# Fox attention scores with zero-padded 128-row queries, earlier copies in two queues, and one pool window on VectorE

## The reference

```
z = rmsnorm(x, g_mix) @ w_in            # 512 q, 512 k, 512 v, 512 pool columns, 8 forget columns
q, k: split in 8 heads of 64, each rms-normed with a gain
c = cumsum(log_sigmoid(f_logit))
s[t, u] = q_t . k_u / 8 + c[t] - c[u]   for u <= t, else -inf     (forgetting attention)
fox = softmax(s) @ v
pool, group g of 4 (128 columns each), w = 2, 4, 8, 16:
    mixed = mean of the last w frames - the frame;  y_g = mixed @ w_pool[g] * pool_scale
h = x + concat(fox, y) @ w_out
```

## Time and profile before

| | us |
|---|---|
| median of 3 runs | 1363.58 (1363.48 to 1363.75) |
| the profiled execution, its own time | 1360.7 |
| its span | 1358.9 |
| TensorE busy | 1316.6 |
| VectorE busy | 762.7 |
| ScalarE busy | 651.2 |
| GpSimd busy | 105.1 |

### The profile page before, as it was taken

The page is one execution under the profiler, slowest core; times in us unless marked ns, Lnnn a source line. Parts: engine busy times, 40 slices in busy tenths (PEclk is TensorE's granted clock), DMA queues, the critical chain, the costliest instruction groups (busy, mean ns, idle before and its releaser), DMA issues.

```text
span 1358.9 us, 16931 instructions
## 1 busy us (share of the span) xinstructions
PE 1316.6 (97%) x6139; PEld 1082.6 (80%) x6139; DVE 762.7 (56%) x834; ACT 651.2 (48%) x894; POOL 105.1 (8%) x163
## 2 busy tenths in 40 slices
PE   7999889999999999999999999999999999999998
PEld 5777768888888888788788888788888887788886
DVE  5646465555564455657655555755556557754444
ACT  5554455444454444455644444644445556644443
POOL 5114100000000000110100000200002002100000
PEclk9999999999999999999999999999999999999999
DMA  9423236555555555455465555555556533555551
GB/s 324 167 69 123 93 124 205 188 191 189 186 165 187 192 188 196 159 198 185 141 222 187 188 187 191 183 185 187 185 186 188 186 106 118 173 190 185 185 188 60
DMA packets 163485, 236.02 MB, mean 174 GB/s; under 512 B 7745, under 2 KB 120569, under 8 KB 163441
## 3 DMA queue, kind: packets, MB, share of 16 engines
q1 hardware_dynamic: 160864, 228.62, 51.8%
q0 software_dynamic: 1840, 4.64, 1.0%
q10 hardware_dynamic: 736, 2.17, 0.4%
HBM read 234.35 MB, written 1.05 MB: 173 GB/s over the span
## 4 chain that ended last, share of the span: by engine, by line
PE 89%; DVE 4%; ACT 2%; POOL 2%; issue 1%; DMA 1%; SPq 0%; DVEq 0%; POOLq 0%; ACTq 0%
PE B L1519 20%; PE B L1521 20%; PE B L1520 20%; PE B L1878 7%; PE B L1880 7%; PE B L1879 7%; PE T L1891 2%; DVE w_lo L976 2%; DMA w_raw<-in_w_in 1%; DVE xt_lo L991 1%; ACT w_hi L527 1%; POOL KT L414 1%; PE B L2048 1%; PE T L1513 0%; ACT xt_hi L540 0%
## 5 line engine op out<-in xcount | busy, mean ns | idle before, releaser
L976 DVE TENSOR_TENSOR w_lo<-w_raw,w_hi 128x2048 fp32r<-128x2048 f32 x217 | 498.7, 2299 | 296.8 <-ACT w_hi L527 296.8
L527 ACT ACTIVATE w_hi<-w_raw 128x2048 fp32r<-128x2048 f32 x217 | 415.6, 1916 | 168.6 <-PE B L1880 127.3
L1519 PE MATMUL B<-w_hi,xt_lo 128*128 128x512 f32 x1200 | 479.5, 400 | 8.8 <-DVE xt_lo L991 4.7
L1521 PE MATMUL B<-w_hi,xt_hi 128*128 128x512 f32 x1200 | 469.1, 391 | 0.0
L1520 PE MATMUL B<-w_lo,xt_hi 128*128 128x512 f32 x1200 | 468.0, 390 | 0.0
L1519 PEld LDWEIGHTS B<-w_hi,xt_lo 128*128 128x128 f32 x1200 | 225.9, 188 | 56.7 <-issue 8.5
L1521 PEld LDWEIGHTS B<-w_hi,xt_hi 128*128 128x128 f32 x1200 | 225.7, 188 | 48.6
L1520 PEld LDWEIGHTS B<-w_lo,xt_hi 128*128 128x128 f32 x1200 | 226.3, 189 | 43.7
L1878 PE MATMUL B<-w_hi,act_lo 128*128 128x512 f32 x400 | 156.3, 391 | 0.0
L1880 PE MATMUL B<-w_hi,act_hi 128*128 128x512 f32 x400 | 155.7, 389 | 0.0
L1879 PE MATMUL B<-w_lo,act_hi 128*128 128x512 f32 x400 | 155.6, 389 | 0.0
(11 more groups left out here) (269 smaller groups left out, 898.3 us busy)
## 6 DMA issues: line engine op xcount, KB each, us to landing
w_raw<-in_ffn_w_gu SPq DMA_DIRECT2D x176, 512.0 KB, 4.6
w_raw<-in_ffn_w_down SPq DMA_DIRECT2D x88, 512.0 KB, 3.9
w_raw<-in_w_gate_up SPq DMA_DIRECT2D x44, 512.0 KB, 4.7
w_raw<-in_conv_w_in SPq DMA_DIRECT2D x24, 512.0 KB, 4.3
w_raw<-in_w_down SPq DMA_DIRECT2D x22, 512.0 KB, 3.8
w_raw<-in_w_in SPq DMA_DIRECT2D x16, 512.0 KB, 7.9
w_raw<-in_w_kv SPq DMA_DIRECT2D x16, 512.0 KB, 4.9
w_raw<-in_w_mem_kv SPq DMA_DIRECT2D x8, 512.0 KB, 4.7
```

The lines of the kernel that those rows point to most:

```text
L527: act.activation(whi[slot][:, :], raw[slot][:, :], ACT.Copy).then_inc(w_hi, 1)
L976: dve.tensor_tensor(wlo[slot][:, :], raw[slot][:, :], whi[slot][:, :].bitcast(F32), ALU.subtract)\
L1519: pe.matmul(bank[:, :], lo[:, k, x], whi[s][:, c], start=first, stop=False)
L1521: return pe.matmul(bank[:, :], hi[:, k, x], whi[s][:, c], start=False, stop=last)
```

## The change

- QT now holds all eight chunks for the Fox heads: chunk `2 c + m` has head `2 c + m` in its own 64 rows and zeros in the others. VectorE writes the zeros at the start; the later zeroing of the same places for the differential attention stays, and its counts on `qz_ok` are 2 higher. `fox_scores` multiplies 128 rows of padded queries by the 128 rows of KT that hold both heads of a pair.
- The queries are taken out by two instructions per engine, each for half of the partitions, and these stand directly behind the evacuation of the keys.
- TensorE makes two fill triples between the scores of heads 0 and 1.
- ScalarE and VectorE take the pool columns out ahead of split 9; ScalarE's squares of the memory rows stand at heads 2 and 3.
- mixT moves to `gpost`, so the first load of `gpost` comes later in GpSimd's queue. The window of 16 frames is made by VectorE (`widest_window`), at i = 4.
- VectorE scales the memory keys behind the attention output.

```diff
...
 win = [kt_hi[:, (PAD + S) * i:(PAD + S) * (i + 1)] for i in range(2)]
+win16 = [Z[:, i, 2 * (PAD + S):3 * (PAD + S)] for i in range(2)]
 wmean = kt_hi[:, 2 * (PAD + S):2 * (PAD + S) + S]
-mixT = QT[:, 4:8, :]
+mixT = gpost[:, :].rearrange("p (g t) -> p g t", g=4)
 
...
 mixed_ok, py_done = sem("pool_mixed"), sem("pool_product")
+mixed16_ok, pads16_ok = sem("widest_window_mixed"), sem("widest_window_pads_zero")
 at_s, at_m, at_x, at_e, at_r, at_c, at_v = (sem("scores_done"), sem("scores_masked"), sem("row_max_ready"),
...
 
-        if b:
-            pool.wait_ge(h_up, 4 * (3 + b - 1) + 4)
+        pool.wait_ge(*((h_up, 4 * (3 + b - 1) + 4) if b else (py_done, 1)))
         pool.dma_start(gpost[:, :], a["norm_g_2"][layer, i].partition_broadcast(P)).then_inc(post_in, 16)
...
         pool.wait_ge(pads_ok, 3)
-        for g, w in enumerate(WINDOWS):
+        for g, w in enumerate(WINDOWS[:3]):
             src = poolT[g]
...
 
-    post_gain(0, 0, 1)
     row_stat("h0")
...
     row_stat("h2")
+    post_gain(0, 0, 1)
     row_stat("h3")
...
         act.activation(dst, FILL[0][:, :], ACT.Copy, scale=RS[:, ST[stat], 0:1]).then_inc(ev_a, 1)
+
+    def fox_queries_out():
+
+        act.wait_ge(ht, 2 * HT_QF + 1)
+        act.wait_ge(qz_ok, 2)
+        for m in range(2):
+            r = slice(m * FOX_DH, m * FOX_DH + FOX_DH)
+            ins = act.activation(qz_g[0][r, m, 0:2, :], T[0][r, :].rearrange("p (c t) -> p c t", c=2), ACT.Copy,
+                                 scale=gains[r, G_QF:G_QF + 1])
+        ins.then_inc(ht_a, 1)
 
...
     evac(EV_IN + 1, 3, Z[:, 0, 512:1024], PAIR[1], "h0")
+    act.wait_ge(gain_ok, 6)
+    fox_queries_out()
     head_square(1, Z[:, :, 512:1024], EV_IN + 1)
     split_at(6)
-    act.wait_ge(gain_ok, 6)
-    heads_out(HT_QF, QT[:, 0:2, :], G_QF)
     mem_round_hi(0)
...
             mem_round_hi(3)
+            fill_evac(0, Z[:, 0, 1024:1536], "h0")
             split_at(9)
-            mem_squares(0)
-            mem_squares(1)
-            fill_evac(0, Z[:, 0, 1024:1536], "h0")
         elif i == 2:
             split_at(10)
+            mem_squares(0)
             act.wait_ge(pt_done, 1)
...
         elif i == 3:
+            mem_squares(1)
             split_at(11)
...
     dve.memset(gains[:, G_ONE:G_ONE + 1], 1.0).then_inc(gain_ok, 1)
+    dve.memset(qz_g[0][FOX_DH:P, 0], 0.0).then_inc(qz_ok, 1)
+    dve.memset(qz_g[0][0:FOX_DH, 1], 0.0).then_inc(qz_ok, 1)
...
         dve.tensor_scalar(dst, FILL[1][:, :], RS[:, ST[stat], 1:2], None, ALU.mult).then_inc(ev_d, 1)
+
+    def widest_window():
+
+        src = poolT[3]
+        for level in range(4):
+            d = 1 << level
+            dst = win16[level % 2]
+            link(dve.tensor_tensor(dst[:, PAD:PAD + S], src[:, PAD:PAD + S], src[:, PAD - d:PAD + S - d], ALU.add))
+            src = dst
+        dve.scalar_tensor_tensor(out=mixT[:, 3, 16:S], in0=src[:, PAD + 16:PAD + S], scalar=1.0 / WINDOWS[3],
+                                 in1=poolT[3][:, PAD + 16:PAD + S], op0=ALU.mult, op1=ALU.subtract)
+        link(dve.tensor_tensor(src[:, PAD:PAD + 16], src[:, PAD:PAD + 16], cnt16[:, 3, :], ALU.mult))
+        dve.tensor_tensor(mixT[:, 3, 0:16], src[:, PAD:PAD + 16], poolT[3][:, PAD:PAD + 16], ALU.subtract)\
+            .then_inc(mixed16_ok, 1)
 
...
     evac(EV_IN + 1, 3, Z[:, 1, 512:1024], PAIR[1], "h0")
+    dve.wait_ge(ht, 2 * HT_QF + 2)
+    for m in range(2):
+        r = slice(m * FOX_DH, m * FOX_DH + FOX_DH)
+        ins = dve.tensor_scalar(qz_g[0][r, m, 2:4, :], T[1][r, :].rearrange("p (c t) -> p c t", c=2),
+                                gains[r, G_QF:G_QF + 1], None, ALU.mult)
+    ins.then_inc(ht_d, 1)
     head_sum(1, FOX_H, FOX_DH)
     split_at(6)
-    heads_out(HT_QF, QT[:, 2:4, :], G_QF)
     head_scale(1, Z[:, :, 512:1024], FOX_H, FOX_DH)
...
         elif i == 1:
+            fill_evac(U_IN + 7, Z[:, 1, 1024:1536], "h0")
             split_at(9)
-            fill_evac(U_IN + 7, Z[:, 1, 1024:1536], "h0")
         elif i == 2:
...
                 .then_inc(pt_out, 1)
+            for w in win16:
+                dve.memset(w[:, 0:PAD], 0.0).then_inc(pads16_ok, 1)
         elif i == 4:
+            dve.wait_ge(pt_out, 2)
+            dve.wait_ge(pads_ok, 3)
+            dve.wait_ge(pads16_ok, 2)
+            widest_window()
             fill_evac(U_MEMKV + 1, nat[:, 1, HALF:D], "mem")
...
             split_at(13)
-            head_scale(2, nat[:, :, HALF:D], MEM_H, MEM_DH)
             dve.wait_ge(pool_hi, 4)
...
     values_out(0, 16, 0, FOX_H, FOX_DH)
+    head_scale(2, nat[:, :, HALF:D], MEM_H, MEM_DH)
     split_at(14)
...
     def fox_scores(i):
-        c, r = i // 2, slice(64 * (i % 2), 64 * (i % 2) + 64)
+        c, q = i // 2, qz_g[0][:, i % 2, i // 2, :]
         if i >= 2:
...
         b = B[i % 2]
-        for q, lo, width in ((0, 0, P), (1, P, S)):
-            pe.matmul(b[:, lo:lo + width], QT[r, c, q * P:q * P + P], KT[r, c, 0:width], start=True, stop=False)
+        for t, lo, width in ((0, 0, P), (1, P, S)):
+            pe.matmul(b[:, lo:lo + width], q[:, t * P:t * P + P], KT[:, c, 0:width], start=True, stop=False)
             ins = pe.matmul(b[:, lo:lo + width], selr[i // 4][:, i % 4, :], cT[:, 0:width], start=False, stop=True)
...
     fox_scores(0)
+    fill(3, 5)
     fox_scores(1)
-    fill(3, 6)
+    fill(5, 6)
     done = 6
...
         if i == 7:
-            pe.wait_ge(mixed_ok, 4)
+            pe.wait_ge(mixed_ok, 3)
+            pe.wait_ge(mixed16_ok, 1)
             pe.wait_ge(in_small, 64)
```

More of the change, by code:

```diff
@@ L480, in _ @@
             pool.memset(qz_g[0][DIFF_DH:P, 0], 0.0).then_inc(qz_ok, 1)
-            pool.wait_ge(qz_ok, 1)
+            pool.wait_ge(qz_ok, 3)
             pool.memset(qz_g[0][0:DIFF_DH, 1], 0.0).then_inc(qz_ok, 1)
-            pool.wait_ge(qz_ok, 2)
+            pool.wait_ge(qz_ok, 4)
             row_stat("h6")
@@ L495, in _ @@
             pool.memset(qz_g[1][DIFF_DH:P, 0], 0.0).then_inc(qz_ok, 1)
-            pool.wait_ge(qz_ok, 3)
+            pool.wait_ge(qz_ok, 5)
             pool.memset(qz_g[1][0:DIFF_DH, 1], 0.0).then_inc(qz_ok, 1)
-            pool.wait_ge(qz_ok, 4)
+            pool.wait_ge(qz_ok, 6)
             for p in range(4):
@@ L869, in queries_out @@
                 act.wait_ge(ht, 2 * (HT_QD + g) + 1)
-                act.wait_ge(qz_ok, 2 * g + 2)
+                act.wait_ge(qz_ok, 2 * g + 4)
                 for m in range(2):
@@ L1379, in queries_out @@
                 dve.wait_ge(ht, 2 * (HT_QD + g) + 2)
-                dve.wait_ge(qz_ok, 2 * g + 2)
+                dve.wait_ge(qz_ok, 2 * g + 4)
                 for m in range(2):
```

## The result

| | before | after |
|---|---|---|
| median of the runs, us | 1363.53 (1360.56 to 1363.75, 4 runs) | 1347.08 (1345.53 to 1347.95, 4 runs) |
| ratio | | 0.9881, 95% interval 0.9856 to 0.9905 |
| profiled execution, us (span, mean granted clock) | 1360.7 (1358.9, 0.998) | 1346.8 (1345.0, 0.997) |

The kernel is 16.5 us faster by the medians. Between the two profiled executions the difference is 13.9 us; the sum had 13.5. The direction was right, and the sum came close by errors that offset each other; what failed is the step from the profiled execution to the median, and one term was mis-sized (W).

What follows compares the result with a forecast made beforehand. TensorE, busy 97% of the span, bounds the kernel. 2.7 + 6.2 + 3.1 + 1.6 + 0.4 + 1.0 - 1.5 = 13.5 us off 1360.7 gives 1347.2, median 1350.1; own range 1348.5 to 1352, stated range 1347.5 to 1355.0.

Steps and rivals of the forecast that it cites:

- W: Added TensorE wait for the memory key bank copy, behind VectorE's window sum: 1.5 us lost, bounds 0 and 4.
- term D: Iteration 2, from 83.21 us: no clock fall once the 3.11 us idle stretch ahead goes, 1.6 us gained, bounds 0 and 1.7.
- A: Fox query copies moved directly behind the key evacuation: TensorE's gap before 50.70 goes, 2.7 us, bounds 1.5 and 2.9.
- C: Value copy moved ahead of the weight split: TensorE's gap before 83.21 goes, 3.1 us, bounds 2.3 and 3.3.
- B: Fox score matmuls on 128 padded rows: 0.80 us a head, 0.72 in the first two, 6.2 us, bounds 0 and 6.6.
- the count of units: Gap before 83.21: the needed split, unit 8's, ends at 63.7, so TensorE waits for ScalarE's value copy, not the labelled split.
- E: Pool product: its wait for GpSimd's fourth window group goes as VectorE takes that group, 0.4 us, bounds 0 to 0.4.
- F: Loop end: memory key scaling moved behind the attention output shortens the gap before 124.17, 1.0 us, bounds 0.5 to 1.1.
- rival 1: VectorE's window: engines interleave without cost or VectorE goes first, so no added wait, 1348.6 us; chance 15%.
- the lock: VectorE's window beside GpSimd's: each holds the other up for nearly the whole instruction, making 2.7 us into 4.7.
- a change of length behind 130 us: Sign of being wrong: work after the Fox loop changes length, where everything behind was to shift as one.

Runs made afterwards that it cites:

- the paired order: Changed kernel with 64-row score matmuls, ordered so that the two 64-row ones of a head stand side by side: 1348.4 us (1348.0 to 1349.1).

## Why the prediction was right in direction, and too high by 3 us

- **The base, the step that failed.** "1347.2 for its like, and for the median of 1363.58, which is 2.9 above it, 1350.1." The 2.9 was carried over as if it were a property of the measurement. It is a property of the kernel before: 61 of its 74 executions have a lower mean clock than the one that my profile showed, and a second profile has a low stretch behind 2.71 us that the first lacks. The changed kernel's runs span 2.4 us (8 executions) instead of 8. Its median is 0.3 above its profile, so 2.6 of the 3.0 us of error lie here. The clock was hence worth the 1.6 of term D in the profile that I had, and some 2.6 more in the median. Which edit brings the 2.6 is open: A and C close the gaps of 2.71 and 3.11, but filling the first alone in the kernel before changed nothing beyond noise (0.9996, 0.9984 to 1.0008). The prediction reasoned that "the gap of 2.71 had none behind it"; one execution could not show that.
- **A** 2.7, measured 2.9 in the traces (47.65 against 50.70, less 0.2 of start). Behind it 0.2 came back: from the turn of the keys at 55.05 to the next product pass 0.99 us against 0.79 before, and VectorE's copy of the sums of logarithms is over at 55.94, 0.10 ahead of that product. The forecast had named this wait, with 0.1. Right; with clock it is worth 5.5 in the new order.
- **B** 0.80 a head by rows 7 and 8, measured 0.73 (5.8 in all against 6.2). Right in kind, 8% too much. The Trainium skill ("TensorEngine Tiling (Array Packing)", section "Key Properties") says that changing the tiling mode drains the array; the runs agree in so far as each change costs 0.19 us. Its "Theoretical Speedup" for contractions of 64 rows or less was not tested: no run had matmuls on both halves of the rows at once.
- **C and D** 4.7, measured 4.9. Right, and the count of units against the label was right.
- **E** 0.4, measured 0.6 (14.08 less 13.48). Right in these traces, but without the move the gap would now be 4.9: the sum gave to A, B and C what was partly the window's.
- **F** 1.0, measured 1.0 by the gap (1.31 to 0.32), but not from F: undone, it changes nothing. The gap closed because GpSimd's norm came early enough, which the window's move brought here. The number was right by luck.
- **W** 1.5, measured 0: rival 1, at 15%, by its number; the engines did hold each other up, by 1.1 us. Two sizes were off. The room from the start of the window to TensorE's need was 4.56 us (91.35 to 95.91) where I had 3.9. The need was 4.32 (91.35 to 95.67) where I had 5.45, since the lock was priced from a row of 2048 columns and one of a different pair of instructions. The Trainium skill ("SBUF — State Buffer", section "SBUF: two separate sides") calls it an exclusive lock for the whole instruction. By the runs the two engines' 256-column additions ran side by side at least in part (four of VectorE in 2.82 us, while GpSimd was busy for 2.5), VectorE's 1.6 times as long and GpSimd's 0.67 against 0.61. Beside the 2048-column split GpSimd did stand for nearly all of it (3.25 us for two additions), so the measurement agrees with the rule for the split and differs for the short additions, and there it decides.
- **What no term had**: the low stretch at 152 us, 1.3 us given back, behind gaps that did not change. Why it comes there is open. The prediction named "a change of length behind 130 us" as a sign that it was wrong, and this is one.

The sum on the profiled executions thus came out by luck, through offsets: W +1.5, A, C, D and E +0.6, the wait at the keys -0.2, B -0.4, the new low stretch -1.3, and 0.2 of start.

## What to carry to other kernels

Look at the runs' own spread and clock before adding an offset between a profiled execution and a median: if the kernel before has idle gaps of some 3 us on TensorE, its spread may be stretches at 1.2 GHz, and a change that closes the gaps may win that too. Price an edit in the order of instructions that the whole change makes, not by the gap it closes in the trace of before: here one edit was worth 6.8 us behind a gap of 0.42, and the largest term of the sum was worth nothing by itself. Where two engines meet, take the price from instructions of the same length as those that will meet.

## What the runs showed of the hardware

- Between a 64-row matmul and one of 72 or 128 rows pass about 0.19 us more than between two of a kind; 72 beside 128 rows shows no such cost (the paired order has 72 to 128 rows at both ends).
- VectorE's addition of 256 columns with two SBUF inputs takes 0.45 us alone and 0.70 beside GpSimd's windows; GpSimd's own goes from 0.61 to 0.67. A 2048-column VectorE split holds a GpSimd addition for about 2 us.
- TensorE's granted clock fell to the 1.2 GHz level for 3.4 to 7.5 us in or behind every single gap from 3.1 to 4.9 us in the stage of the change (3.09, 3.10, 3.11, 3.47, 3.48, 3.65, 3.82 twice, 4.07, 4.89), behind the gap of 2.71 in one profile of two, behind the gap of 2.23 in one of 17, behind three gaps of 0.8 to 1.6 us in a row in some executions, and once with no gap shown in the 20 us ahead. A low stretch costs 1.7 us where TensorE has no gaps (4 us at 0.57), 1.3 in the memory attention, and 3.4 where it is twice as long.
- At the start every profile has a gap of 3.7 to 4.6 us that ends at 9 to 10 us, with a granted clock of 1.00 behind it, yet there the products step 0.43 us (12.42 to 12.85 after the change) where they step 0.23 later. So a granted clock of 1.00 at the start does not show full speed.
